# Value products of an attention loop for two query tiles at a time, with the values stationary, in a new order of rows

## The reference, cut to what matters

```python
q = rms_norm(q, q_norm_g[l])
k = rms_norm(k, k_norm_g[l])
# in blocks of 128 queries, h a head, c one of its two maps
s = jnp.einsum('bhcqd,bhckd->bhcqk', q_blk, kh).astype(jnp.float32) * scale
s = jnp.where(mask, s, NEG_BIG)
p = jax.nn.softmax(s, axis=-1)
w = p[:, :, 0] - lam * p[:, :, 1]
out = jnp.einsum('bhqk,bhke->bhqe', w, vh)
a = rms_norm(a, subln_g[l]) * (1.0 - lam_init)
```

## Time and profile before

| what | value |
|---|---|
| median of 3 runs | 1260.45 us (1260.07 to 1261.19) |
| the profiled execution | 1261.12 us |
| its span, first to last instruction | 1259.3 us |
| TensorE busy, matmuls | 1243.6 us, 99% |
| VectorE busy | 939.8 us, 75% |
| ScalarE busy | 556.5 us, 44% |
| GpSimd busy | 146.9 us, 12% |
| granted TensorE clock | 1.0 of full speed |

### The profile page before, as it was taken

One profiled execution on the slowest core, in us unless ns is written; L12 is line 12 of the kernel. 1 busy time (PEld: TensorE's weight loads), 2 busy tenths in 40 slices (PEclk: granted clock), 3 DMA queues, 4 the chain that ended last, 5 costly groups with the idle time before them and its releaser, 6 DMA issues.

```text
span 1259.3 us, 16180 instructions
## 1 busy us (share of the span) xinstructions
PE 1243.6 (99%) x5885; PEld 1021.7 (81%) x5885; DVE 939.8 (75%) x1316; ACT 556.5 (44%) x961; POOL 146.9 (12%) x198
## 2 busy tenths in 40 slices
PE   9999999998999999999999999999999999999999
PEld 6877877777888888888887888888888888888887
DVE  5547785777998678774578777777778988879864
ACT  5436665656654323322345445355354433333330
POOL 3113322322400040000000000000000000000035
PEclk9999999999999999999999999999999999999999
DMA  7100120112375466422314543544559644363223
GB/s 272 34 17 18 48 61 22 39 34 62 123 243 183 163 205 219 166 101 84 110 41 142 176 148 136 176 142 143 176 205 366 231 167 168 100 232 102 100 92 143
DMA packets 110354, 169.75 MB, mean 135 GB/s; under 512 B 5806, under 2 KB 55875, under 8 KB 110276
## 3 DMA queue, kind: packets, MB, share of 16 engines
q1 hardware_dynamic: 110274, 168.72, 39.1%
q10 hardware_dynamic: 2, 0.00, 0.0%
HBM read 118.37 MB, written 50.33 MB: 134 GB/s over the span
## 4 chain that ended last, share of the span: by engine, by line
PE 86%; DVE 7%; ACT 3%; issue 2%; DMA 1%; SPq 0%; POOL 0%; DVEq 0%; ACTq 0%
PE bank L2263 80%; PE bank L2403 2%; PE bank L2384 1%; DVE small L1558 1%; PE bank L2343 1%; DVE slot_lo L1476 1%; PE bank L2334 1%; DMA x_tile<-in_x 1%; DVE w_tok L1576 1%; DVE c L2163 1%; DVE pair_lo L2057 1%; DVE wT_lo L1542 1%; PE bank L2613 1%; DMA gate_store<-out_tile 1%; ACT prob L1048 0%
## 5 line engine op out<-in xcount | busy, mean ns | idle before, releaser
L2263 PE MATMUL bank<-o_hi,s_lo 128*128 128x512 f32 (+1 forms) x452 | 175.0, 387 | 0.0
L2263 PE MATMUL bank<-o_hi,s_hi 128*128 128x512 f32 (+1 forms) x452 | 175.0, 387 | 0.0
L2163 DVE TENSOR_TENSOR c<-bank,c 128x512 f32<-128x512 f32 x112 | 75.7, 689 | 35.6 <-PE bank L2263 33.9
L2263 PE MATMUL bank<-featT_hi,pair_hi 128*128 128x512 f32 x256 | 99.9, 390 | 0.8 <-DVE c L2163 0.6
L2263 PE MATMUL bank<-o_lo,s_hi 128*128 128x512 f32 (+1 forms) x260 | 100.3, 386 | 0.0
L2263 PE MATMUL bank<-featT_lo,pair_hi 128*128 128x512 f32 x256 | 99.6, 389 | 0.0
L2263 PE MATMUL bank<-featT_hi,pair_lo 128*128 128x512 f32 x256 | 99.6, 389 | 0.0
L2263 PEld LDWEIGHTS bank<-o_hi,s_lo 128*128 128x128 f32 x452 | 84.9, 188 | 17.5
L2263 PEld LDWEIGHTS bank<-o_hi,s_hi 128*128 128x128 f32 x452 | 84.9, 188 | 17.3
L1444 ACT ACTIVATE s_hi<-s_raw 128x2048 fp32r<-128x2048 f32 x28 | 53.7, 1917 | 93.8 <-DMA s_raw<-u_store 93.8
L1420 ACT ACTIVATE c<-c 128x512 f32<-128x512 f32 x64 | 40.0, 624 | 118.9 <-DVE c L2163 118.9
(11 more groups left out here) (283 smaller groups left out, 3166.0 us busy)
## 6 DMA issues: line engine op xcount, KB each, us to landing
s_raw<-u_store SPq DMA_DIRECT2D x28, 1024.0 KB, 5.6
pair_raw<-in_w_mlp_in SPq DMA_DIRECT2D x16, 1024.0 KB, 5.8
u_store<-s_tile SPq DMA_DIRECT2D x64, 256.0 KB, 2.1
o_raw<-in_w_mlp_out SPq DMA_DIRECT2D x16, 1024.0 KB, 8.4
u_store<-u_tile SPq DMA_DIRECT2D x48, 256.0 KB, 2.4
gate_store<-out_tile SPq DMA_DIRECT2D x32, 256.0 KB, 2.4
gate_raw<-in_w_in SPq DMA_DIRECT2D x8, 1024.0 KB, 5.4
raw<-in_w_in SPq DMA_DIRECT2D x12, 512.0 KB, 4.7
```

Source lines behind the costliest of these rows:

```text
L2163: nc.vector.tensor_tensor(out[:], psum, other[:], ALU.add).then_inc(up_sum, 1)
L2263: mm = nc.tensor.matmul(out, a, b, start=start and i == 0, stop=stop and i == len(steps) - 1, skip_group_check=onto)
```

## The change

Values become stationary and the weights moving. For a pair of query tiles (2q, 2q+1 in the new row order) and each key tile k, `v_hi` meets `wT_hi` and `wT_lo`, and `v_lo` meets `wT_hi`, each with 256 moving columns, 128 of either query tile. For the last key tile only the second query tile moves (128 columns). `wT` is one buffer of 12 blocks per part: 8 for the even row, 4 for the odd. The output comes out transposed (value columns on partitions, tokens along the free axis), already summed over the three parts.

It is copied to `out_t` and transposed (`output_turn`), so that ScalarE can square it per token; GpSimd makes the scale of both tiles at once; `scale_spread` transposes that column, broadcast over 128 columns, to have the scale on every partition; VectorE multiplies `out_t` by it (`output_norm`), ScalarE rounds, VectorE takes the rest.

The row order becomes head 0 tiles 0 and 1, head 1 tiles 0 and 1, head 0 tiles 2 and 3 and so on. The second tile of a pair is thus needed one row sooner, and the filler is moved one row ahead (six parts before row 0). Turns of q and k are in rows with g%4 of 0 and 3. On VectorE `qk_lo` and `qk_sum` move from ahead of the mask to behind the first `row_max`.

```diff
-        wT = [both(f"wT{c}", 120 + 4 * c, [P, 4, P], 2) for c in range(2)]
+        wT = both("wT", 116, [P, 12, P], 6)
...
-        W_LAG, O_LAG, SUM_LAG, N_LAG = 2, 3, 4, 5
-        ALL_ROWS = ROWS + N_LAG
+        ROW_PAIRS = ROWS // 2
+        W_LAG, O_LAG, N_LAG = 2, 3, 4
+        ALL_ROWS = ROWS + N_LAG + 1
...
-            return u // 2 % T
+            return u // 4 * 2 % T + u % 2
...
-            return 2 * (u // (2 * T)) + u % 2
+            return 2 * (u // (2 * T)) + u // 2 % 2
...
+        def pair_at(g, lag):
+
+            return g - lag >= 0 and g - lag < ROWS and (g - lag) % 2 == 1
...
-            return g < ROWS and g % 2 == 1 and g // 2 + 1 < STEPS
+            return g < ROWS and g % 4 in (0, 3) and turn_of(g) < STEPS
...
+        def takes_at(g):
+
+            return g < ROWS and g % 2 == 1 and take_of(g) < STEPS
+
+        def take_of(g):
+
+            return g // 2 + 2
...
-            s, odd = divmod(g, 2)
-            if s >= STEPS - 2:
-                return [("first", 4 * (g - 2 * (STEPS - 2)) + i) for i in range(4)]
+            if g >= ROWS - 4:
+                return [("first", 4 * (g - ROWS + 4) + i) for i in range(4)]
+            last = [("qk", KD * (STEPS - 1) + i) for i in range(KD)] + [("x", 2 * KD * GROUPS - KD + i) for i in range(KD)]
+            if g >= ROWS - 7:
+                return last[0:6] if g == ROWS - 7 else last[6:11] if g == ROWS - 6 else last[11:]
+            s, odd = divmod(g + 1, 2)
...
-        POOL_ROWS = (2, 6, 10, 12, 16, 20, 24, 26)
-        POOL_W_ROWS = (8, 14, 22)
+        POOL_ROWS = (1, 5, 9, 11, 15, 19, 23, 27)
+        POOL_W_ROWS = (6, 14, 20)
+        QK_W_ROWS = (11, 12)
...
-        FIRST_W_ROWS = (28, 30, 31, 32)
+        FIRST_W_ROWS = (27, 29, 30, 32)
...
+            def output_scale(q):
+
+                inverse_root(a_ss, VDIM, a_ms, a_rstd, 2, a_squared, 2 * q + 2, a_mean, q + 1, a_inv)
+                pool.wait_ge(a_inv, q + 1)
+                pool.tensor_tensor(a_ms, a_rstd, recip_pair(q), ALU.mult).then_inc(a_scaled, 1)
...
+            def output_copy(q):
+
+                act.wait_ge(out_full, 3 * q + 1)
+                wait(act, out_free, q)
+                nc.scalar.activation(out_t[:], bank[:, OUT, 0:2 * P], ACT.Copy).then_inc(out_copied, 1)
+
+            def output_square(q):
+
+                act.wait_ge(out_full, 3 * q + 2)
+                wait(act, a_mean, q)
+                for i in range(2):
+                    wait(act, a_squared, 2 * q + i)
+                    nc.scalar.activation(o_square[:], bank[:, OUT, (2 + i) * P:(3 + i) * P], ACT.Square,
+                                         scale=recip[(2 * q + i) % 8][:, 0:1], accum_out=a_ss[:, i:i + 1]).then_inc(a_squared, 1)
...
+            def output_norm(q):
+
+                dve.wait_ge(out_full, 3 * q + 3)
+                nc.vector.scalar_tensor_tensor(attn_f[:], out_t[:], sub_scale, bank[:, OUT, 2 * P:4 * P], ALU.mult,
+                                               ALU.mult).then_inc(out_free, 1)
...
+            def attend(g):
+
+                if rows_at(g, O_LAG) and tile_of(g - O_LAG) >= 4:
+                    weights_lo(g - O_LAG, 1)
+                if g % 4 == 2 or g >= ROWS:
+                    split_weights(g)
                 if g < ROWS:
                     mask_diagonal(g)
                     row_max(0, g)
+                if turns_at(g):
+                    qk_lo(turn_of(g))
+                if takes_at(g):
+                    qk_sum(take_of(g))
+                if g < ROWS:
                     row_max(1, g)
+                if g % 4 != 2 and g < ROWS:
+                    split_weights(g)
                 if rows_at(g, W_LAG):
                     weights_lo(g - W_LAG, 0)
-                if rows_at(g, O_LAG) or rows_at(g, N_LAG):
-                    output_sum(g - O_LAG)
+                if pair_at(g, N_LAG):
+                    output_norm(pair_of(g, N_LAG))
                 if g < ROWS:
-                    if not odd and 2 <= s + 1 < STEPS:
-                        qk_norm(s + 1)
+                    if takes_at(g):
+                        qk_norm(take_of(g))
                     coefficients(g)
                     weights(g)
+                if pair_at(g, N_LAG):
+                    output_lo(pair_of(g, N_LAG))
...
+            def outputs(q, c):
+
+                h, t = head_of(2 * q), tile_of(2 * q)
...
+                for k in range(4 * c, min(t + 2, 4 * c + 4)):
+                    two = slice(k, 9 + k % 4, 8 + k % 4 - k) if k <= t else slice(8 + k % 4, 9 + k % 4)
+                    cols = slice(0 if k <= t else P, 2 * P)
+                    v = [v_tok[:, h, k, i, :] for i in range(2)]
+                    for i, (a, b) in enumerate(((v[0], wT[0]), (v[0], wT[1]), (v[1], wT[0]))):
+                        mm = nc.tensor.matmul(k4(bank[:, OUT, cols], 1 + (k <= t)), a, b[:, two, :],
+                                              start=k == 0 and i == 0, stop=k >= t and i == 2, skip_group_check=True)
...
+            def scale_spread(q):
+
+                pe.wait_ge(a_scaled, q + 1)
+                for i in range(2):
+                    mm = nc.tensor.transpose(bank[:, OUT, (2 + i) * P:(3 + i) * P],
+                                             a_ms[:, i:i + 1].to_broadcast([P, P]), ident[:])
+                mm.then_inc(out_full, 1)
+
             def attend(g):
 
                 parts = fill_of(g) if g < ROWS else [("first", KD * (g - ROWS + 2) + k) for k in range(KD)]
...
+                if g < ROWS:
+                    scores(g)
+                if turns_at(g) and g != ROWS // 2:
+                    qk_transpose(turn_of(g))
+                if pair_at(g, N_LAG):
+                    output_turn(pair_of(g, N_LAG))
+                middle = 4 if g >= ROWS else 3 if turns_at(g) else 2 if g % 2 == 1 else 0
+                fill(parts[0:middle])
+                if turns_at(g) and g == ROWS // 2:
+                    qk_transpose(turn_of(g))
+                if pair_at(g, O_LAG):
+                    q = pair_of(g, O_LAG)
+                    outputs(q, int(tile_of(2 * q) >= 4))
                 if rows_at(g, W_LAG):
                     weights_transpose(g - W_LAG, 0)
+                if pair_at(g, N_LAG):
+                    fill(parts[middle:middle + 2])
+                    scale_spread(pair_of(g, N_LAG))
+                    middle += 2
                 fill(parts[middle:])
+                if pair_at(g, W_LAG) and tile_of(g - W_LAG) >= 4:
+                    outputs(pair_of(g, W_LAG), 0)
                 if rows_at(g, W_LAG) and tile_of(g - W_LAG) >= 4:
                     weights_transpose(g - W_LAG, 1)
...
+            fill(fill_of(-1))
             for g in range(ALL_ROWS):
                 attend(g)
```

More of the change, by code:

```diff
@@ L228, in trunk_layer @@
         coef = sm(68)
-        a_ss, a_ms, a_rstd = sm(69), sm(70), sm(71)
-        a_scale = [sm(72 + i) for i in range(2)]
+        a_ss, a_ms, a_rstd = sm(69, 2), sm(71, 2), sm(73, 2)
         lam_diff = sm(75)
@@ L384, in v_bank, with w_place, recip_pair, attn_place @@
             return POOLED + t % 2
+        def w_place(u, c, n):
+            k0 = 4 * c if u % 2 == 0 else 2 * 4
+            return slice(k0, k0 + n)
+        def recip_pair(q):
+            a = (92, 96, 64, 116)[q % 4]
+            return small[:, a:a + 3:2]
+        def attn_place(q):
+            h, t = head_of(2 * q), tile_of(2 * q)
+            if h < 2:
+                return attn_kept[:, 0, :], attn_kept[:, 1, :]
+            return tuple(part[:, t * P:(t + 2) * P] for part in attnT[h])
         FIRST_W = 4 * HEADS + 1
@@ L758, in _ @@
             store_c11(7)
-            for i in range(2):
-                sp.wait_ge(attn_out[i], 16 * T)
+            sp.wait_ge(attn_out, 16 * T)
             for h in range(2):
@@ L972, in _ @@
             for g in range(ALL_ROWS):
-                if rows_at(g, SUM_LAG):
-                    output_scale((g - SUM_LAG) % 4, g - SUM_LAG)
-                if g < ROWS and g % 2 == 0 and 2 <= g // 2 + 1 < STEPS:
-                    qk_inverse(g // 2 + 1)
+                if pair_at(g, N_LAG):
+                    output_scale(pair_of(g, N_LAG))
+                if takes_at(g):
+                    qk_inverse(take_of(g))
             wide_sums(3, range(3))
@@ new lines, in output_square, with output_hi @@
+            def output_square(q):
[5 more added lines that the diff above has]
+                                         scale=recip[(2 * q + i) % 8][:, 0:1], accum_out=a_ss[:, i:i + 1]).then_inc(a_squared, 1)
+            def output_hi(q):
+                act.wait_ge(out_free, q + 1)
+                if head_of(2 * q) < 2:
+                    wait(act, attn_out, 16 * q)
+                nc.scalar.activation(attn_place(q)[0], attn_f[:], ACT.Copy).then_inc(attn_hi, 1)
@@ L1764, in side_add @@
                 elif n == 4:
-                    for i in range(2):
-                        dve.wait_ge(attn_out[i], 16 * T)
```

(34 more changed lines are left out.)

184 lines of the change are left out of this document (70 added, 114 removed).

## The result

| | before | after |
|---|---|---|
| median | 1260.74 us (1260.07 to 1261.19, 4 runs) | 1269.13 us (1268.29 to 1270.15, 4 runs) |
| span of the profiled execution | 1259.3 us | 1267.1 us |

The changed kernel is slower: ratio 1.0067, 95% interval 1.005 to 1.0085. The forecast was 1253.8.

What follows compares the result with a forecast made beforehand. TensorE was taken as the bound, with 12.5 us of real waits in the attention loop. Work -1.9, old waits -10.0 and new waits +5.2 gave -6.7 us from 1261.12: 1254.4, as median 1253.8 (range 1250 to 1257.5, chance 0.55).

Steps and rivals of the forecast that it cites:

- old waits: Attention loop: of 12.5 us of real TensorE waits, the new orders leave 2.5, so -10.0 us.
- (a): Odd rows: first projection waits for bank PROJ, read twice by qk_take, where value products lay before; +2.1 us.
- (b): Steps taken in rows 3, 7, 19, 23 are turned in the very next row, too soon for qk_normed; +2.1 us.
- scale chain: New wait (c): scale_spread waits 3.0 us for ScalarE and GpSimd, TensorE issues 3.1 to 3.4 meanwhile; even, +1.0 for jitter.
- TensorE work: Attention loop's net issue: value products -5.4 us, output and spread transposes +3.5, together -1.9.
- cover of 0.5 us: Behind the loop: last side_lo ends at 360.18, its product can start at 360.7, so the loop's gain is kept.
- New waits, +5.2: Attention loop: waits made by the new order, (a) +2.1, (b) +2.1 and (c) +1.0 us.
- (c): The scale chain's wait at scale_spread on TensorE: even, with +1.0 us for jitter over 16 pairs.
- The slower rival: TensorE waits for GpSimd's slow small operations, 0.7 us more per pair: 1264.0 us; chance 0.11, shared with costly value products.
- moved waits: Rival: order only changes who is late, old and new waits sum to about 12 us; 1258.6 us, chance 0.17.

Runs made afterwards that it cites:

- e4: Kernel before with the new row order, projections one row ahead, new weight rows and VectorE's new order, but old value products and norm: 1260.16 us.
- e1: Changed kernel with ScalarE's two output squares moved ahead of the weight splits of the same row: 1264.69 us.
- e3: Kernel before with VectorE's new order alone (mask and first row maximum ahead of qk_lo and qk_sum): 1269.85 us.
- e12: e7 with VectorE's old order put back (qk_lo and qk_sum ahead of the mask): 1259.88 us.
- e7: e4 with ScalarE's first exponential ahead of its weight rounding in rows that turn q and k and from row 27 on: 1254.60 us.
- e13: e7 with the changed kernel's order of side sums, the fourth made to wait for the last value products: 1256.44 us.
- e14: e11 without the output norm (no out_t transposes, squares, scale or spread; output scaled by the gains alone): 1257.14 us.
- e10: e1 with the spread one part earlier and one filler part ahead of the c=1 value products in rows 10, 14 to 30: 1265.00 us.
- e11: e10 with ScalarE's first exponential ahead of its weight rounding in rows that turn q and k and from row 27 on: 1263.63 us.

## Why the prediction was wrong

**The sum by its two halves.** The forecast gave -5.8 us to the orders of rows and engines (-10.0 of old waits, +4.2 of new ones under (a) and (b)) and -0.9 to the value products (-1.9 of work, +1.0 for the scale chain). Against their own before, e4, which has the orders alone, measured -1.0, and the changed kernel +8.4. So the orders missed by 4.8 us, and the value products, at +9.4, by 10.3: 4.9 of the 9.4 went with the squares (e1), 4.5 stayed.

**TensorE work, -1.9: right.** A value product of 256 columns costs 0.12 (193.00 to 193.12). Narrow ones start 0.087 us apart on average behind another narrow one and 0.11 ahead of a transpose, so the 240 come to about 27.6 us, for 27.4 in the forecast (my estimate from these spacings). The spread's transposes start 0.11 apart, as assumed. The counts fit too: by the forecast's prices e1 issues 2.0 us less than e4 (195.26 and 46.26 against 196.51 and 46.97).

**Old waits, -10.0: the step that failed.** It read VectorE's 28.0 us of idle time before `qk_lo` as time on the path. e3 takes it to 3.5 us and costs 8.7. The idle time was slack before an operation that TensorE needs early, for the bank TB; the work put into it delayed that operation, and in row 13 TensorE stood still for 3.58 us, with 6.8 us at half clock that began 1.7 us before it went on. Only with the new row order and the exponential first is the same order a gain (e12, 5.3 us). The forecast priced the order by itself, in the wrong surroundings. In e4, with all the orders, the gaps of rows 0 to 30 are 24.9 us for 25.5 before. The maxima, moreover, weren't what held the exponentials in turn rows of the new row order: ScalarE's wait for the transposed weights was (e7). The forecast read that wait, 49.0 us in the earlier trace rows, and then left it alone.

**The value products' place: not in the sum, and this failed by more.** The forecast let the halved products shorten the old waits and put nothing down for their own. They bring three costs instead: waits of their own, of the second half in rows 14, 18 and 30 for the rest of its weights (2.5 us) and of the first half in rows 27, 29 and 31 for `attn_f` (2.4 us); the tail of the loop; and 1.6 us in the gates by the side sums (shown by e13), where the forecast took its cover of 0.5 us for enough. Together the value half costs about 9 us with the best orders found. Of this, 1.6 are shown by e13, and e14 excludes the norm's chain as the cause of the rest; rows 11 to 18 hold 4.8 us of it by the count, rows 27 to 30 2.0 and the tail 1.8, less the 1.9 of saved issue: with the gates 8.3 of the 9.0. That the transposes of the same step are the cause from row 27 on is read from the waits (row 29 of e14 among them); no edit tests it. For rows 11 to 18 the cause isn't settled; 1.8 us there, in row 14, come from the edit of e10, which took away the second half's waits and left the time as it was.

**New waits, +5.2.** (a) PROJ in row 1 showed as forecast, a wait of 0.63 (0.7 forecast), and in row 17 0.64 (0.9). (b) The quick turns cost 0.5 us or more in rows 7, 8, 23 and 24 of e4, as forecast in size; their cause was ScalarE's order, since e7 takes them away. In the changed kernel rows 8 and 24 have 0.33 each. (c) The scale chain: no wait in 12 of 16 pairs, as forecast, 0.2 in row 27, but 2.1 us in row 11 and 1.1 twice in the tail, 4.6 in all for 1.0, since ScalarE's squares stood behind weight splits, which the working of 3.0 us had left out.

**The slower rival** (scale chain, 1264.0) had its sign right, and its mechanism in one row only: it wanted waits in most pairs. The Trainium skill, page "SBUF — State Buffer", section "SBUF: two separate sides", has its rule of the port lock borne out in row 11 (1.55 us for a power beside `slot_lo`, 0.70 for the same one in e1; with the operation ahead of it, 0.67 for 0.19, that is 1.3 of the 2.13 us). But e1, without any wait for GpSimd, is still 3.5 us slower than before, so the late chain, its stalls in the tail and the half clock in its wake are 4.9 of the 8.4 us. One reading behind the rival was wrong: the 0.19 us operation at 95.39 ran beside a `w_tok`, which starts at 95.39 too and takes 0.49, and not beside reductions from PSUM. The rival *moved waits* came nearest in kind: the changed kernel has 31.5 - 13.0 = 18.5 us beside issue and switching, more than before, not the 12 it gave.

## What to carry to other kernels

Idle time before an operation is worth filling only if that operation isn't what others wait for: ask who needs its result and when, then test the order alone before adding it up. A new producer or consumer gets its own waits as a term of the sum, even where the guess is nothing. Price an operation that is moved nearer to its producer by the whole chain (transpose, round, rest) against the work that is left in that row, the shortest rows first. An order on one engine has no price of its own: the same one cost 8.7 us in one row order and gained 5.3 in another, so edits that touch the same hand-over are measured together and apart.

## What the hardware showed that I had not expected

Short stalls of TensorE were followed by half clock. Idle 2.13 us in row 11 of the changed kernel: 3.4 us at 0.50 from 1.2 us later on. Idle 3.58 us in e3: 6.8 us at 0.50, from 1.9 us after the stall began. In e1 idle times of 0.81 and 0.95 us close behind each other came before 3.4 us at 0.50, and the changed kernel has the same two at 1.00. It isn't regular: the same wait of 1.82 us in row 14 was followed by half clock in e10 and e14 (row 14 took 10.6 us) and not in e11 (9.09). In this loop a stall could cost nearly twice its length: 2.1 + 1.7 us in row 11.

It differs between executions of one kernel too. Of e10's seven, the two with a mean granted clock of 1.000 took 1263.0 and 1263.5 us, three at 0.999 took 1264.5 to 1265.5, and two at 0.997, of which the profiled one has two such stretches, 1266.0 and 1266.6. So one stretch of 3.4 us goes with 1 to 2 us here, and differences of that size between two medians of this document can be the clock's.
